# Layer 1's last two feed-forward parts as seven block products on 256-token blocks, with the weight sums on GpSimd

## The reference

```python
h2 = modulate(rms_norm(x, norm2_g[l]), sh2, sc2)
x = x + gt2 * swiglu(h2, w_ffn_gate[l], w_ffn_up[l], w_ffn_down[l])
# swiglu(h, g, u, d) = (silu(h @ g) * (h @ u)) @ d
```

## Time and profile before

| what | us |
|---|---|
| median of 3 runs (lowest, highest) | 2407.94 (2406.51, 2411.88) |
| profiled execution, its own time | 2408.51 |
| its span in the trace | 2406.7 |
| PE busy | 2324.5 |
| DVE busy | 1646.8 |
| ACT busy | 1187.9 |
| POOL busy | 219.9 |

### The profile page before, as it was taken

The page is one execution under the profiler, slowest core; times in us unless marked ns, Lnnn a source line. Parts: engine busy times, 40 slices in busy tenths (PEclk is TensorE's granted clock), DMA queues, the critical chain, the costliest instruction groups (busy, mean ns, idle before and its releaser), DMA issues.

```text
span 2406.7 us, 32940 instructions
## 1 busy us (share of the span) xinstructions
PE 2324.5 (97%) x12159; PEld 1987.5 (83%) x12159; DVE 1646.8 (68%) x2529; ACT 1187.9 (49%) x1906; POOL 219.9 (9%) x335
## 2 busy tenths in 40 slices
PE   7999999999999999999999999999999999999899
PEld 3888887888888998998778777898888877877687
DVE  5786776789687877878686777754333466389864
ACT  4647777733333431432647776343222355477541
POOL 0100000020001112221100000100000010011020
PEclk9999999999999999999999999999999999999999
DMA  7421111174333237337221111523222333521253
GB/s 289 147 79 47 47 47 44 48 274 155 112 125 139 107 110 247 129 142 253 100 88 53 49 53 67 183 80 105 96 97 96 105 109 132 182 90 64 83 201 119
DMA packets 71381, 282.41 MB, mean 117 GB/s; under 512 B 9040, under 2 KB 9104, under 8 KB 69824
## 3 DMA queue, kind: packets, MB, share of 16 engines
q1 hardware_dynamic: 42336, 162.94, 19.6%
q0 software_dynamic: 28896, 117.46, 13.9%
HBM read 245.76 MB, written 33.55 MB: 116 GB/s over the span
## 4 chain that ended last, share of the span: by engine, by line
PE 77%; DVE 9%; ACT 7%; issue 4%; DMA 2%; POOL 0%; SPq 0%; ACTq 0%; DVEq 0%
PE ps L217 21%; PE ps L218 21%; PE ps L219 21%; DVE w_lo L213 2%; PE ps L1282 1%; PE ps L1216 1%; PE ps L1283 1%; PE ps L1284 1%; DMA ada_raw<-in_ada 1%; PE ps L1223 1%; ACT w_hi L206 1%; DVE inv L1446 1%; PE ps L1265 1%; ACT pr L1345 1%; DVE maxes L1469 1%
## 5 line engine op out<-in xcount | busy, mean ns | idle before, releaser
L217 PE MATMUL ps<-h_hi,w_hi 128*128 128x512 f32 (+2 forms) x1592 | 576.7, 362 | 16.6 <-DVE h_lo L1585 7.5
L218 PE MATMUL ps<-h_lo,w_hi 128*128 128x512 f32 (+2 forms) x1592 | 566.6, 356 | 0.0
L219 PE MATMUL ps<-h_hi,w_lo 128*128 128x512 f32 (+2 forms) x1592 | 565.6, 355 | 0.0
L213 DVE TENSOR_TENSOR w_lo<-w_raw,w_hi 128x1024 fp32r<-128x1024 f32 x256 | 319.2, 1248 | 190.6 <-ACT w_hi L206 190.4
L206 ACT ACTIVATE w_hi<-w_raw 128x1024 fp32r<-128x1024 f32 x256 | 269.2, 1053 | 235.0 <-PE ps L219 215.5
L217 PEld LDWEIGHTS ps<-h_hi,w_hi 128*128 128x128 f32 x1592 | 302.5, 190 | 67.3 <-issue 15.8
L219 PEld LDWEIGHTS ps<-h_hi,w_lo 128*128 128x128 f32 x1592 | 301.9, 190 | 44.2
L218 PEld LDWEIGHTS ps<-h_lo,w_hi 128*128 128x128 f32 x1592 | 302.6, 190 | 42.5 <-issue 2.4
L217 PE MATMUL ps<-q_hi,w_hi 128*128 128x512 f32 x720 | 255.6, 355 | 1.7 <-DVE q_lo L1606 1.7
L218 PE MATMUL ps<-q_lo,w_hi 128*128 128x512 f32 x720 | 256.3, 356 | 0.0
L219 PE MATMUL ps<-q_hi,w_lo 128*128 128x512 f32 x720 | 254.5, 354 | 0.0
(11 more groups left out here) (446 smaller groups left out, 4276.1 us busy)
## 6 DMA issues: line engine op xcount, KB each, us to landing
w_raw<-in_stream SPq DMA_DIRECT2D x288, 512.0 KB, 3.3
wt_x<-in_ada_t POOLq DMA_DIRECT2D x24, 512.0 KB, 3.7
wt_h<-in_ada_t POOLq DMA_DIRECT2D x20, 512.0 KB, 5.2
ada_raw<-in_ada SPq DMA_DIRECT2D x4, 2048.0 KB, 19.2
wt<-in_ada_t POOLq DMA_DIRECT2D x16, 512.0 KB, 3.8
x_keep<-x POOLq DMA_DIRECT2D x8, 768.0 KB, 7.8
gates<-th_g POOLq DMA_DIRECT2D x16, 384.0 KB, 2.6
gates<-sg POOLq DMA_DIRECT2D x24, 256.0 KB, 2.3
```

Source lines behind the costliest of these rows:

```text
L213: nc.vector.tensor_tensor(w_lo[:, u % 3, :], raw[:, u % 2, :], w_hi[:, u % 3, :].bitcast(F32), ALU.subtract).then_inc(lo_ready, 1)
L217: nc.tensor.matmul(out_ap, lh, rh, start=start, stop=False)
L218: nc.tensor.matmul(out_ap, lh, rl, start=False, stop=False)
L219: return nc.tensor.matmul(out_ap, ll, rh, start=False, stop=stop)
```

## The change

Layer 1's parts become 6, 8, 8 pairs, and its last two parts go through `hidden_pairs` with token blocks of 256 (`half`). Part 0 stays in `hidden_late`. Three things are new:

- `TokenBlocks` makes the four token sums on POOL from `n_hi` + `n_lo` once the eight opening units of part 0 are done (`scaled` at 8, all of `n_lo` written): one addition of 7 x 512 elements, one of 512, and four of 1024 elements. ACT and DVE split the four sums during the first four down units of part 0.
- `PairsAgain` loads each pair's two weight units a second time, by two DMAs on POOL's queue, to one buffer `raw_again`; all three weight sums are POOL's, from that copy. `w_raw` feeds only the blocks that are not sums, so `lo_ready` counts at low 1 and low 5 in place of low 3 and low 5.
- DVE has neither `sum_acd` nor `sum_abcd` in layer 1.

```diff
-FF_PARTS = ((6, 8, 8), (8, 8, 6))
+FF_PARTS = ((6, 8, 8), (6, 8, 8))
...
+            def sums(self, pool, scaled):
...
+                pool.wait_ge(scaled.sem, scaled.base + 8)
+                pool.wait_ge(late.whole_lo.sem, late.whole_lo.base + CH)
+                combine(joined[:, 0:CH - 1, :], late.n_hi[:, 0:CH - 1, :].bitcast(F32), r_kv["n_lo"][:, :, :].bitcast(F32), ALU.add)
+                combine(joined[:, CH - 1, :], late.n_hi[:, CH - 1, :].bitcast(F32), late.n_lo[CH - 1].bitcast(F32),
+                    ALU.add).then_inc(self.joined.sem, 1)
+                pool.wait_ge(self.joined.sem, self.joined.base + 1)
+                combine(f["t1"], f["b11"], f["b12"], ALU.subtract).then_inc(self.summed.sem, 1)
+                combine(f["t3"], f["b22"], f["b12"], ALU.subtract).then_inc(self.summed.sem, 1)
+                pool.wait_ge(self.summed.sem, self.summed.base + 2)
+                combine(f["t2"], f["t3"], f["b11"], ALU.add).then_inc(self.summed.sem, 1)
+                pool.wait_ge(self.summed.sem, self.summed.base + 3)
+                combine(f["t4"], f["t2"], f["b21"], ALU.subtract).then_inc(self.summed.sem, 1)
...
+            def load_again(self, pool, p):
+
+                u = self.base + 2 * p
+                pool.wait_ge(self.summed.sem, self.summed.base + 3 * p)
+                for s in range(2):
+                    pool.dma_start(r_h["raw_again"][:, s, :], stream[u + s]).then_inc(self.again.sem, 16)
+
+            def all_sums(self, pool, p):
+
+                c = self.copy
+                pool.wait_ge(self.again.sem, self.again.base + 32 * (p + 1))
+                pool.wait_ge(self.low.sem, self.low.base + max(4 * p - 1, 0))
+                nc.gpsimd.tensor_tensor(self.sums_tile, c[:, 0:4:3, :], c[:, 2:3, :].to_broadcast([P, 2, 512]),
+                                        ALU.add).then_inc(self.summed.sem, 1)
+                pool.wait_ge(self.summed.sem, self.summed.base + 3 * p + 1)
+                nc.gpsimd.tensor_tensor(self.sums[2], self.sums[0], c[:, 3, :], ALU.add).then_inc(self.summed.sem, 1)
+                pool.wait_ge(self.summed.sem, self.summed.base + 3 * p + 2)
+                pool.wait_ge(self.low.sem, self.low.base + 4 * p)
+                nc.gpsimd.tensor_tensor(self.sums[3], self.sums[2], c[:, 1, :], ALU.add).then_inc(self.summed.sem, 1)
...
             def pool(e):
                 made = 7 + sum(DOWN_PASSES) if part == 2 else 0
+                if not side:
+                    pairs.load_again(e, 0)
+                    for p in range(N):
+                        pairs.all_sums(e, p)
+                        if p + 1 < N:
+                            pairs.load_again(e, p + 1)
+                    return
```

More of the change, by code:

```diff
@@ L1789, in __init__, with high_at, low_at @@
                         self.lo[name], self.full[name] = tiles[7 + k], sums[k]
+            lows, half = 7, HALF
+            second_sign = ALU.add
+            def high_at(self, name, c):
+                return self.hi[name][:, c]
+            def low_at(self, name, c):
+                return self.lo[name][:, c]
             def times(self, dve, c):
@@ L1828, in high_of, with __init__, high_at, low_at @@
                     nc.scalar.activation(self.hi[name], self.full[name], ACT.Copy).then_inc(self.high.sem, 1)
+        class TokenBlocks:
+            ORDER = ("t1", "t3", "t2", "t4")
+            lows, half = 4, SEQ // 2
+            second_sign = ALU.subtract
+            def __init__(self, late, base):
+                self.late, self.base = late, base
+                self.joined, self.summed, self.high, self.low = signals("norm", scaled=1, summed=4, high=4, low=4)
+                tiles, sums = r_h["token_blocks"], r_h["token_sums"]
+                self.hi = {name: tiles[:, n] for n, name in enumerate(self.ORDER)}
+                self.lo = {name: tiles[:, 4 + n] for n, name in enumerate(self.ORDER)}
+                self.full = {name: sums[:, 4 + n] for n, name in enumerate(self.ORDER)}
+                left, right = slice(0, self.half), slice(self.half, SEQ)
+                self.place = {"b11": (0, right), "b12": (0, left), "b21": (4, right), "b22": (4, left)}
+                for name, (c, cols) in self.place.items():
+                    self.full[name] = r_h["rejoined"][:, c:c + 4, cols]
+            def high_at(self, name, c):
+                if name in self.hi:
+                    return self.hi[name][:, c]
+                first, cols = self.place[name]
+                return self.late.n_hi[:, first + c, cols]
+            def low_at(self, name, c):
+                if name in self.lo:
+                    return self.lo[name][:, c]
+                first, cols = self.place[name]
+                return self.late.n_lo[first + c][:, cols]
+            def sums(self, pool, scaled):
+                f, late, joined = self.full, self.late, r_h["rejoined"]
+                combine = nc.gpsimd.tensor_tensor
+                pool.wait_ge(scaled.sem, scaled.base + 8)
[10 more added lines that the diff above has]
+                combine(f["t4"], f["t2"], f["b21"], ALU.subtract).then_inc(self.summed.sem, 1)
+            def high_of(self, act, j):
+                if j < 4:
+                    name = self.ORDER[j]
+                    act.wait_ge(self.summed.sem, self.summed.base + j + 1)
+                    nc.scalar.activation(self.hi[name], self.full[name], ACT.Copy).then_inc(self.high.sem, 1)
+            def sums_and_low(self, dve, j):
+                if j < 4:
+                    name = self.ORDER[j]
+                    dve.wait_ge(self.high.sem, self.high.base + j + 1)
+                    dve.wait_ge(self.summed.sem, self.summed.base + (1, 3, 4, 4)[j])
+                    nc.vector.tensor_tensor(self.lo[name], self.full[name], self.hi[name].bitcast(F32), ALU.subtract).then_inc(self.low.sem, 1)
@@ L1838, in __init__ @@
                 pairs_at.append((base, n))
-                self.high, self.low, self.summed = signals("heads", high=7 * n, low=5 * n, mixed=3 * n)
+                self.high, self.low, self.summed = signals("heads", high=7 * n, low=self.lows * n, mixed=3 * n)
                 self.sums_tile = r_h["w_sums_h"][:, :, :]
@@ L1974, in wait_here, with hidden_pairs @@
                     dve.wait_ge(self.x_here.sem, self.x_here.base + 16 * (9 + j))
-        def hidden_pairs(pairs, blocks, before, side, spill, part):
+        def hidden_pairs(pairs, blocks, before, side=None, spill=None, part=0):
             nonlocal u0
@@ L2059, in second_sum @@
                     wait_product(p, 2)
[L2060 removed]
+                    nc.vector.tensor_tensor(ff[:, p % 2, left], su[:, p % 2, right], bank(p, 2), blocks.second_sign).then_inc(summed.sem, 1)
                 def gate_right(p):
@@ L2070, in middle_sums @@
                     if at < 7:
-                        ins = nc.vector.tensor_tensor(halves(qf[:, p, :]), ps[:, at:at + 2, 0:HALF], twice_over(ff[:, p % 2, left]), ALU.add)
+                        ins = nc.vector.tensor_tensor(halves(qf[:, p, 0:w]), ps[:, at:at + 2, 0:half], twice_over(ff[:, p % 2, left]), ALU.add)
                     else:
@@ L2081, in ups @@
                     if at < 7:
-                        ins = nc.vector.tensor_tensor(halves(ff[:, p % 2, :]), ps[:, at:at + 2, 0:HALF], twice_over(qf[:, p, left]), ALU.add)
+                        ins = nc.vector.tensor_tensor(halves(ff[:, p % 2, 0:w]), ps[:, at:at + 2, 0:half], twice_over(qf[:, p, left]), ALU.add)
                     else:
@@ L2130, in dve @@
                             gate_right(p)
-                        if k == 0 and (p or part == 2):
+                        if side and k == 0 and (p or part == 2):
                             side.one_pass(e)
@@ L2135, in dve @@
                 hidden_low(N - 1)
-                if part == 1:
+                if side and part == 1:
                     side.wt_out = su[:, :, :].rearrange("p a n -> p (a n)")[:, 0:D]
@@ L2250, in act @@
                         late.whole_high(e, c)
-                    if blocks and 4 <= n < 12:
+                    if blocks and not late.whole and 4 <= n < 12:
                         blocks.shift(e, n - 4)
@@ L2289, in dve @@
                         late.times(e, c)
-                    if blocks and 3 <= n < 11:
+                    if blocks and not late.whole and 3 <= n < 11:
                         blocks.times(e, n - 3)
@@ L2295, in pool @@
             def pool(e):
+                if late.whole:
+                    blocks.sums(e, scaled)
+                    return
                 e.wait_ge(late.low.sem, late.low.base + CH + 1)
@@ L3214, in build_program @@
             banks, late = None, norm
-            blocks, pairs, spill = (Blocks(norm), None, Spill()) if layer == 0 else (None, None, None)
+            blocks, pairs, spill = (Blocks(norm), None, Spill()) if layer == 0 else (TokenBlocks(norm, u0), None, None)
             for part, nf in enumerate(FF_PARTS[layer]):
@@ L3223, in build_program @@
```

(2 more changed lines are left out.)

89 lines of the change are left out of this document (67 added, 22 removed).

## The result

| | before | after |
|---|---|---|
| median of the runs | 2407.28 us (4 runs, 2406.5 to 2411.9) | 2422.96 us (4 runs, 2421.6 to 2429.7) |
| profiled execution | 2408.5 us, span 2406.7 | 2423.3 us, span 2421.5 |
| PE / DVE / POOL busy | 2324.5 / 1646.8 / 219.9 us | 2322.3 / 1770.9 / 353.4 us |

The account below looks back on a forecast made before the run. PE, busy 97% of the span, was taken as the bound, with POOL's round of load and sums setting the new pairs' period. 2408.5 - 12.8 + 5.5 + 7.2 = 2408.4, brought to the median 2407.8 us; range 2398 to 2415.

Parts of the forecast that it names:

- step 3: Part 0's long POOL addition of 7 x 512 elements holds the port 8.0 us; PE stalls 5.5 us near 1639.
- step 4: Pairs of layer 1's last two parts: POOL's load and sums set a period of 11.5 us, losing 3.6 a part, 7.2.
- Step 1: PE in layer 1's pairs: 10.08 us a pair instead of 10.88, over 16 pairs 12.8 us less.
- Step 2: SBUF port shared by POOL and DVE: one waits out the other's instruction; POOL takes 2.42 us for 1024 elements.
- rival B: Part 0's long addition does not hold the port, so no stall: 2402.3 us, chance 0.12.
- A1: Time within a part when pair 1's sum a+c+d is ready: about 6.0 us.
- product 2: Block product of a pair that PE can start 2.0 us after a+c+d; pair 7's due at 73.4, forecast at 77.0.
- A6: Time within a part when pair 6's sum a+c+d is ready, forecast as 63.5 us.
- rival C: Pairs: load of 5.9 us or more, double low before POOL's 1024 sum; 8.4 us lost a part, 2417.4, chance 0.18.
- Step 5: Work under cover, free: first pair's copy and sums, token blocks' highs and lows during down units, added DMA traffic.
- rival A: Pairs: POOL keeps up, period under 11.1 us, 0 to 1.2 lost a part; 2400.6 us with 0, chance 0.23.

Follow-up runs that it names:

- e4: Changed kernel with POOL's three sums of every pair but each part's first cut to 8 of 512 columns, second load kept; 2405.56 us, ratio 0.9987.
- e3: Changed kernel with a second buffer for POOL's copies of the weights, so each pair's load starts a pair earlier; 2421.57 us, ratio 1.0054.
- e1: Changed kernel with part 0's one POOL addition of 7 x 512 elements written as seven of 512; 2415.99 us, ratio 1.0031.
- e9: Changed kernel with seven short additions in part 0 and all four sums of a pair on VectorE, from one copy buffer; 2398.17 us, ratio 0.9960.
- e7: Kernel before, with only layer 1's parts cut as 6, 8, 8 pairs and ordinary products; 2408.08 us, ratio 1.0002.
- e5: e1 with two copy buffers and all four block sums of a pair moved from POOL to VectorE; 2400.89 us, ratio 0.9973.
- e10: e1 with a+c and c+d made by accumulating DMA and VectorE's two sums reading copies of b and d, second session; 2403.37 us, ratio 0.9977.

## Why the prediction was wrong, step by step

The two losses were sized too small: part 0 at 5.5 us, where it cost 10.7 (step 3), and the pairs at 7.2, where they cost 18.9 (step 4). That is 16.9 us too little, the whole of the miss (15.2 us by the medians).

- **Step 1, PE.** Right: 0.120 us apart, 12.8 us less (e4 runs both parts at exactly this pace).
- **Step 2, who may read SBUF.** Right, up to a length of 7.9 us that no row had shown, in both directions: PSUM operands go free (e3), SBUF operands wait to the end. By the rule of the Trainium skill that the prediction weighed (SBUF — State Buffer, "Who interferes with whom") the other engine blocks for the whole instruction; the 8.46 us agree, over a length at which no row of before could say so.
- **Step 3, the long sum.** The mechanism was right, e1 shows it, and rival B is out; the size was 10.7 and not 5.5. Of the 5.2 us missing, 2.3 are the stall, 7.8 for 5.5. The forecast let ff pass before POOL and had one 1.31 us addition slip between; in fact POOL and ff were released by the same instruction, POOL got the port although its row starts 0.05 us later, ff took 7.7 us more than its own 0.75, and then q_lo and w_lo each gave a turn to one of POOL's additions, w_lo to one of 1024 elements (2.68 us). The other 2.9 us are the clock, a term that the forecast put at nothing: "no clock term arises" was read from a stretch without gaps, and did not hold once the forecast itself put a gap in.
- **Step 4, the pairs.** The period was nearly right, 11.5 forecast and, between the first round and the last, 11.4 to 11.7 seen in part 1 and 11.6 to 12.3 in part 2, with the order of turns as forecast in all but one; and A1 = 6.0 came at 6.2. The loss, 3.6 forecast and 9.2 seen in part 1, was built up from it wrongly: one period for all rounds, the wait looked for at product 2 alone, and no clock. The first matmul of the last pair started at 78.2 us after the part's first, where PE's own pace gives 70.6; the forecast's timeline has it at A6 + 10.2 = 73.7. Of the 4.5 us between, 3.1 are A6 (66.6 for 63.5), nearly all of it in the first period of 14.3, when the load took 6.5 us in place of the 4.5 to 4.7 of later ones; between 1700 and 1710 the DMA engines moved 2.1 MB, this 1 MB and as much of the weights', and the load shared over 5 us with weight loads where the later ones shared some 2. 1.4 are the turns: at the ring's end the double low is two single ones, 3.95 us with two of POOL's sums let in. Then 1.5 us at the lower clock behind that gap. Part 2 has the same terms (a first load of 5.9 us, 1.5 us of slow matmuls) and the one round in rival C's order. A slow load was taken for a constant with a small chance, rival C, when in this profile it was the first load inside each part (6.5 and 5.9 us) and none of the other five, which took 4.5 to 4.8. That the result lies near C's 2417.4 is luck: C's condition, a load of 5.9 us or more in every round, didn't hold.
- **The bound.** The forecast said that the period is "set by POOL's round of load and sums with the port turns in it". For the kernel as it stands that is what the chain shows. It is only half the cause, and that the number came out is in part luck: e3 takes the load out of the way, and DVE, with its 3.9 us of held instructions, has a period of its own of 11.6. The argument that the forecast put down against rival A, that little overlap leaves DVE near 11, was the stronger mechanism. e4 and e9 separate the two: the load stays in both, and it costs nothing there. Rival A is out by the same figures: but for the last one of each part no round was under 11.4 us.
- **Step 5.** Free but for 0.1 us, as said (e7 for the parts, e4 for the DMA traffic).

That the gaps of some 2.2 us in the pairs brought the lower clock (0.79 granted from 1768 to 1776) is read from the rows and wasn't tested by itself; e1 had one of 2.5 us at 1760.5 behind which no matmul was slow (1.00 from 1763 to 1768), so the length of the gap alone doesn't decide it. Why POOL won the first turn in part 0 was not tested either.

## What to carry to other kernels

Before work goes to GpSimd, price what it takes from VectorE: here each sum of 512 elements on GpSimd held VectorE's instructions for about 1 us (e3, 3.9 us for the four of a pair), and VectorE makes the same sum in 0.65 (e5, 2.65 us for the four), so giving them to the idle engine was a loss, and taking them back won some 17 us (e1 to e9, 1.0031 to 0.9960). Where GpSimd must work beside VectorE, give it short instructions, so that a late low part waits for one of them and not for all. And when a chain of waits shows one round, look whether a second engine is full at the same period: removing the round alone then gives nothing.

## What the runs showed that was not expected

- Where both had work that reads two operands from SBUF, GpSimd and VectorE took turns one by one. In e1 seven additions of 512 elements, 1.3 us each when alone, took 12.11 us among VectorE's instructions, and each of those with two SBUF operands waited for one addition.
- TensorE's granted clock was 0.55 in the 11 us from inside the 7.8 us gap on, and behind it matmuls came 0.32 to 0.59 us apart in place of 0.2267 for 6.0 us. It happened behind some gaps of 2.1 to 2.3 us in the pairs also (some 1.5 us each time), and not behind others of that length.
- An accumulating transfer into SBUF from GpSimd's queue works as a sum that takes nothing of VectorE and 1.2 us of GpSimd's queue, but here it had to wait until the plain load had landed; with six blocks a pair GpSimd once waited 10 us for that, and VectorE's sum began 8.5 us later (e10).
